# Where the output rows and the fast tiles of a feed-forward lie: two more tiles of each by Strassen's method, row products in equal units

## The reference, cut to what matters

```python
def swiglu(h, w_gate, w_up, w_down):
    return (jax.nn.silu(h @ w_gate) * (h @ w_up)) @ w_down

for l in range(2):
    x = x + 0.5 * swiglu(rms_norm(x, ffn1_norm[l]), ffn1_wg[l], ffn1_wu[l], ffn1_wd[l])
    ...                         # mixing stage
    x = x + 0.5 * swiglu(rms_norm(x, ffn2_norm[l]), ffn2_wg[l], ffn2_wu[l], ffn2_wd[l])
```

## Time and profile before

| | |
|---|---|
| median of 3 runs | 2541.45 us (2541.44 to 2541.8) |
| the profiled execution | 2541.64 us, its span 2539.8 us |
| TensorE busy | 2519.7 us, 13626 matmuls |
| weight loads busy | 2177.9 us |
| VectorE busy | 1834.5 us |
| ScalarE busy | 1143.8 us |
| GpSimd busy | 303.9 us |
| read from HBM | 241.84 MB |
| TensorE's granted clock | 1.000 of full speed |

### The profile page before, as it was taken

The page is one execution under the profiler, slowest core; times in us unless marked ns, Lnnn a source line. Parts: engine busy times, 40 slices in busy tenths (PEclk is TensorE's granted clock), DMA queues, the critical chain, the costliest instruction groups (busy, mean ns, idle before and its releaser), DMA issues.

```text
span 2539.8 us, 34207 instructions
## 1 busy us (share of the span) xinstructions
PE 2519.7 (99%) x13626; PEld 2177.9 (86%) x13626; DVE 1834.5 (72%) x2475; ACT 1143.8 (45%) x1771; POOL 303.9 (12%) x250
## 2 busy tenths in 40 slices
PE   8999999999999999999999999999999999999999
PEld 7899988888999889999888899997888888788887
DVE  8877767777778677776776777777999786642433
ACT  5434445444434454443553444445577535431332
POOL 4000001320000000000023000000186231100001
PEclk9999999999999999999999999999999999999999
DMA  5333333233333333333423333234332333233332
GB/s 154 99 101 93 97 102 92 75 101 90 103 97 100 109 97 95 95 112 93 108 59 100 92 88 110 86 112 127 84 74 75 125 91 109 83 108 100 91 100 83
DMA packets 488421, 248.27 MB, mean 98 GB/s; under 512 B 40385, under 2 KB 485062, under 8 KB 488006
## 3 DMA queue, kind: packets, MB, share of 16 engines
q1 hardware_dynamic: 487810, 245.76, 33.5%
q10 hardware_dynamic: 452, 0.32, 0.1%
HBM read 241.84 MB, written 4.19 MB: 97 GB/s over the span
## 4 chain that ended last, share of the span: by engine, by line
PE 95%; DVE 3%; ACT 1%; issue 0%; DMA 0%; POOL 0%; DVEq 0%; ACTq 0%
PE bank L704 8%; PE bank L706 8%; PE bank L705 8%; PE bank L785 6%; PE bank L784 6%; PE bank L783 6%; PE psS L804 6%; PE psS L805 6%; PE psS L806 6%; PE psT L704 4%; PE psT L705 4%; PE psT L706 4%; PE psT L870 2%; PE psT L872 2%; PE psT L871 2%; PE psS L704 1%
## 5 line engine op out<-in xcount | busy, mean ns | idle before, releaser
L2004 DVE TENSOR_TENSOR wlo<-raw,whi 128x1024 fp32r<-128x1024 f32 (+1 forms) x274 | 362.0, 1323 | 114.8 <-ACT whi L1422 111.6
L704 PE MATMUL bank<-xhi,whi 128*128 128x512 f32 x888 | 349.3, 393 | 1.5 <-issue 1.5
L705 PE MATMUL bank<-xlo,whi 128*128 128x512 f32 x888 | 345.9, 390 | 0.0
L706 PE MATMUL bank<-xhi,wlo 128*128 128x512 f32 x888 | 345.8, 389 | 0.0
L1422 ACT ACTIVATE whi<-raw 128x1024 fp32r<-128x1024 f32 (+1 forms) x271 | 277.4, 1026 | 131.9 <-PE psT L706 92.4
L1454 ACT ACTIVATE whi<-tw 128x1024 fp32r<-128x1024 f32 x112 | 119.0, 1062 | 234.4 <-PE bank L785 205.8
L804 PE MATMUL psS<-hhi,whi 128*128 128x512 f32 x512 | 201.7, 394 | 0.0
L805 PE MATMUL psS<-hlo,whi 128*128 128x512 f32 x512 | 201.5, 394 | 0.0
L806 PE MATMUL psS<-hhi,wlo 128*128 128x512 f32 x512 | 199.2, 389 | 0.0
L704 PEld LDWEIGHTS bank<-xhi,whi 128*128 128x128 f32 x888 | 166.8, 188 | 36.8 <-issue 2.9
L705 PEld LDWEIGHTS bank<-xlo,whi 128*128 128x128 f32 x888 | 166.7, 188 | 35.1 <-issue 1.4
(11 more groups left out here) (596 smaller groups left out, 6498.6 us busy)
## 6 DMA issues: line engine op xcount, KB each, us to landing
raw<-in_ffn_wg SPq DMA_DIRECT2D x88, 512.0 KB
raw<-in_ffn_wu SPq DMA_DIRECT2D x88, 512.0 KB
raw<-in_ffn_wd SPq DMA_DIRECT2D x96, 384.0 KB
raw<-in_w_mlp SPq DMA_DIRECT2D x64, 512.0 KB
raw<-in_w_in SPq DMA_DIRECT2D x53, 512.0 KB
raw<-in_ffn_wd SPq DMA_DIRECT2D x32, 256.0 KB
raw<-in_w_in SPq DMA_DIRECT2D x24, 256.0 KB
raw<-in_w_out SPq DMA_DIRECT2D x11, 512.0 KB
```

Source lines behind the costliest of these rows:

```text
L704: pe.matmul(dest, a, rhs_hi(k), start=start and k == 0, stop=False)
L705: pe.matmul(dest, a, rhs_lo(k), start=False, stop=False)
L706: mm = pe.matmul(dest, b_, rhs_hi(k), start=False, stop=stop and k == tiles - 1)
L2004: dve.tensor_tensor(wlo[:, a:a + n], raw[:, a:a + n], whi[:, a:a + n].bitcast(F32), ALU.subtract).then_inc(s_split, 1)
```

## The change

The list of windows goes. The three plain windows stay (tiles 0 to 5), and each of the other 16 tiles has a fast window: FAST = 16 instead of 14, no mixed ones. GROUPS become 6, 6, 5 and 5 tiles. The output rows of a group are laid out as one list of blocks (row by row, one 128 x 128 block of weights each), and `down_units` cuts that list into equal units, two for each window of the next group: 4 blocks a unit while group 0 and group 2 are worked off, 4 or 5 for group 1. So a row can begin in the middle of one unit and end in another, a row's bank of `psS` is chosen by m % 2 instead of by unit, and a unit that holds parts of two rows is loaded by two transfers. The waits for hidden tiles and for free banks move to single blocks, and a row is added where it ends. The last group has 5 tiles, so each row of `last_down` has 5 blocks where it had 6.

```diff
-    WINDOWS = [("plain", 0, None), ("plain", 2, None), ("plain", 4, None)]
-    GROUPS = [(0, 6), (6, 12), (12, 16), (16, FC)]
-    WINDOWS += [("mixed", 6, None)] + [("down", 8 + i, (0, 2 * i)) for i in range(KC // 2)]
-    WINDOWS += [("down", 12 + i, (1, 2 * i)) for i in range(KC // 2)]
-    WINDOWS += [("down", 16, (2, 0)), ("down", 17, (2, 2)), ("mixed", 18, None), ("down", 20, (2, 4)), ("down", 21, (2, 6))]
+    GROUPS = [(0, 6), (6, 12), (12, 17), (17, FC)]
+    FAST = FC - 2 * PLAIN
+
+    def down_units(grp, n):
+        rows = [(grp, m, k) for m in range(KC) for k in range(GROUPS[grp][1] - GROUPS[grp][0])]
+        return [rows[len(rows) * i // n:len(rows) * (i + 1) // n] for i in range(n)]
+
+    SIDES = []
+    for grp, (f0, f1) in enumerate(GROUPS[1:]):
+        units = down_units(grp, 2 * (f1 - f0))
+        SIDES += [units[2 * i:2 * i + 2] for i in range(f1 - f0)]
...
+        def side_cols(w, i):
+            return len(SIDES[w][i]) * P
+
+        def side_ends(w, i):
+            return [(grp, m) for grp, m, k in SIDES[w][i] if k == tiles_in(grp) - 1]
...
+                def side_rows(w, i):
+                    c = c0 + 4 * (PLAIN + w) + 2 + i
+                    slot_free(c, q0)
+                    unit = SIDES[w][i]
+                    chunks = sorted({(grp, m) for grp, m, k in unit})
+                    at_k = 0
+                    for grp, m in chunks:
+                        ks = [k for g_, m_, k in unit if m_ == m]
+                        k0 = GROUPS[grp][0] + ks[0]
+                        sp.dma_start(dst(c, at_k, at_k + len(ks)), cols(wd, l, k0, k0 + len(ks), m * P)
+                                     ).then_inc(landed[slot(c)], LANDED // len(chunks))
+                        at_k += len(ks)
...
-                def side_half(w, i, half, dest):
-                    kind, tile, side = WINDOWS[w]
-                    n = 4 if kind == "mixed" else tiles_in(side[0]) // 2
-                    for k in range(half * n, (half + 1) * n):
...
+                def side_half(w, i, half):
+                    unit = SIDES[w][i]
+                    cut = (len(unit) + 1) // 2
+                    for j in (range(cut, len(unit)) if half else range(cut)):
+                        grp, m, k = unit[j]
+                        if k == 0:
+                            if grp or m >= 2:
+                                pe.wait_ge(k_xa, nf * ADDS + grp * KC + m - 1)
+                            elif m == 0:
+                                pe.wait_ge(s_gs, fb + 2 * PLAIN)
+                        if m == 0:
+                            pe.wait_ge(s_hl, fb + GROUPS[grp][0] + k + 1)
+                        a, dest = (2 * i + 1) * UNIT + j * P, psS[:, m % 2 * S:(m % 2 + 1) * S]
+                        at_h, last = (GROUPS[grp][0] + k) % HT, k == tiles_in(grp) - 1
+                        pe.matmul(dest, whi[:, a:a + P], chunk(hhi, at_h), start=k == 0, stop=False)
+                        pe.matmul(dest, whi[:, a:a + P], chunk(hlo, at_h), start=False, stop=False)
+                        mm = pe.matmul(dest, wlo[:, a:a + P], chunk(hhi, at_h), start=False, stop=last)
                     return mm
...
-                for w, (kind, tile, side) in enumerate(WINDOWS):
-                    if kind == "plain":
-                        pair(q0 + 4 * w, fb + tile, w == 0)
-                    else:
-                        fast_window(w)
+                for w in range(PLAIN):
+                    pair(q0 + 4 * w, fb + 2 * w, w == 0)
+                for w in range(FAST):
+                    fast_window(w)
...
+                def side_adds(w, i):
+                    ends = side_ends(w, i)
+                    if ends:
+                        dve.wait_ge(s_used, q0 + c0 + 4 * (PLAIN + w) + 2 + 2 * i)
+                    for grp, m in ends:
+                        dve.scalar_tensor_tensor(chunk(x, m), psS[:, m % 2 * S:(m % 2 + 1) * S], 0.5, chunk(x, m), ALU.mult,
+                                                 ALU.add).then_inc(k_xa, 1)
```

More of the change, by code:

```diff
@@ L1551, in fast_window @@
                         last_hi(w + 1)
-                    hidden_hi(w, True)
-                for w, (kind, tile, side) in enumerate(WINDOWS):
-                    if kind == "plain":
-                        pair(w)
-                    else:
-                        fast_window(w)
+                    hidden_hi(w)
+                for w in range(PLAIN):
+                    pair(w)
+                for w in range(FAST):
+                    fast_window(w)
                 for m in range(KC):
@@ L2153, in hidden_lo @@
+                def hidden_lo(w):
+                    tile = 2 * PLAIN + w
                     dve.wait_ge(s_hh, fb + tile + 1)
-                    dve.tensor_tensor(chunk(hlo, tile % HT), tmp[3 if fast else 2][:, :], chunk(hhi, tile % HT).bitcast(F32),
+                    dve.tensor_tensor(chunk(hlo, tile % HT), tmp[3][:, :], chunk(hhi, tile % HT).bitcast(F32),
                                       ALU.subtract).then_inc(s_hl, 1)
                 def fast_window(w):
-                    kind, tile, side = WINDOWS[w]
@@ L2159, in fast_window @@
[L2159 removed]
+                    u, g, f = 4 * (PLAIN + w), nf * FAST + w, fb + 2 * PLAIN + w
                     c = q0 + c0 + u
[L2161 removed]
+                    on = w + 1 < FAST
                     t1, t2 = quarter
[L2163 to L2166 removed]
+                    if w:
+                        side_adds(w - 1, 1)
@@ L2167, in fast_window @@
                     whole_lo(w, 1)
-                    if before == "mixed":
-                        hidden_lo(w - 1, False)
                     dve.wait_ge(k_pe, 5 * g + 2)
@@ L2178, in fast_window @@
                         ahead(u + 4)
[L2179 to L2183 removed]
+                    side_adds(w, 0)
                     if on:
@@ L2207, in fast_window @@
                         last_lo(w + 1)
-                    hidden_lo(w, True)
-                for w, (kind, tile, side) in enumerate(WINDOWS):
-                    if kind == "plain":
-                        pair(w)
-                    else:
-                        fast_window(w)
-                side_add(len(WINDOWS) - 1, 1)
+                    hidden_lo(w)
+                for w in range(PLAIN):
+                    pair(w)
+                for w in range(FAST):
+                    fast_window(w)
+                side_adds(FAST - 1, 1)
                 for m in range(KC):
```

159 lines of the change are left out of this document (49 added, 110 removed).

## The result

| | before | after |
|---|---|---|
| median | 2541.59 us (13 runs, 2541.44 to 2542.06) | 2546.93 us (13 runs, 2546.57 to 2548.47) |
| ratio | | 1.0022, interval 1.0014 to 1.0029 |
| the profiled execution | 2541.64 us, span 2539.8 | 2548.21 us, span 2546.4 |

The kernel became 5.3 us slower. The forecast was 2546.7, slower by 5.1. After's runs stand at two levels: 7 of 13 at 2546.57 to 2546.93, 6 at 2548.12 to 2548.47; the profiled execution is one of the upper ones. The median is the highest run of the lower level, so it hangs on that seventh run. What the 1.5 us between the levels are is told with the experiment on it.

The account below looks back on a forecast made before the run. TensorE was taken as the bound, busy 2519.7 of 2539.8 us. Terms -5.76 + 10.6 + 0.2 = +5.1 us on the profiled 2541.64 gave 2546.7 us, 0.2% slower, own range 2545 to 2548, wider range 2543.5 to 2551.

Parts of the forecast that it names:

- Two more tiles by Strassen: In each of four feed-forwards, two plain tiles (10.88 us) become fast ones (10.16); eight tiles save 5.76 us of TensorE.
- Sixteen short windows, none stalls: Fast windows of each feed-forward: eleven at 15.60 us, five at 16.7 on average, nothing stalls, cost nothing.
- Rival C: Fast windows too short for weight transfers and vector work; 0.2 us more over 44 windows gives 2555 us; chance 0.08.
- The first window: First window of the first feed-forward: TensorE arrives 1.36 us sooner, splits shrink, stall stays about 1.6 us; cost 0.
- The tail: Output rows behind each last window: vector engine steps of 3.48, then 4.09 us make TensorE wait; 10.6 us lost in all.
- Behind the tail: Phase after the norm's sum: something with under 0.97 us to spare may lose it, three times; taken as 0.2 us.
- Rival B: Next phase follows the vector engine, losing all of the 0.97 us three times: 2549.4 us; chance 0.15.
- A: Rows behind the last window: vector step under TensorE's 3.40 us, 5.76 us earned in full: 2535.9 us; chance 0.10.
- D: First rows behind the last window overlap better, step 3.3 to 3.4 us, waits vanish: 2542 to 2544 us; chance 0.12.

## Why the prediction was right

*Two more tiles by Strassen, -5.76.* Shown by the three kernels whose tails and windows don't stall: 2535.96, 2536.03 and 2535.93, that is 5.8 to 5.9 us below the kernel before as timed beside each (2541.86, 2541.86 and 2541.76).

*Sixteen short windows, none stalls.* Right in all 64 but the first: 15.60, and 16.69 on average for the five (16.7 predicted). Rival C is wrong here, but near: with groups 6, 5, 5, 6 its wait appears in a window of 14.91 us. The lateness that I read was too small: the 0.28 us of one window became 0.16 to 1.45 us of wait for the up weights in every window but the first and the last of each feed-forward. The slack covered it: in the window from 258.62 VectorE still waits 1.69 us for TensorE, and in the one with 1.45, a window of 16.28 us, 1.19.

*The first window.* The stall was to stay at about 1.6 us, and is 1.66. The window took 17.34, 1.74 above 15.60; the fast windows begin at 79.84, 0.06 later than before.

*The tail.* Right in its steps. The additions' last came at 26.08 (26.09 predicted), row 7 at 18.64 (18.65), chunk 7 at 28.36 (28.39), the norm's sum at 29.17 (29.2). The wait at row 7 was 0.56 where I had 0.69, since TensorE lost 0.13 in restarts on the way and came later; at chunk 7 it was 1.43 (1.5), behind the second feed-forward 2.14 (2.3), with the product that waits for x high starting 27.57 after the first addition (27.6). In sum 10.9 by two runs, where I had 10.6. One reading was wrong without harm to the sum: I wrote that the last three splits are of 1024-column weights, and ahead of the mixing stage half of these columns hold nothing that is used.

*The reason I gave for its pace* was half right. I wrote that VectorE is working off its own chain. With 640 columns that holds within 0.11 us of 3.48; with 1024 columns the circle over ScalarE is as long, and work taken from VectorE buys nothing. The sum came out because its steps were read from the distances of additions, which hold both engines' parts. As a guide to a cure the reason misled: it made me expect 2535.8 of a kernel that took 2560.53.

*Behind the tail, +0.2.* The fast windows of the next three feed-forwards begin 1.12, 4.51 and 5.49 us later than before. By my terms it is 1.09, 2.86 and 3.89; the second has 1.65 more, which is the fallen clock of the profiled execution, and the rest agrees within 0.1. Rival B did not come; 27 us behind the last row of the fourth one TensorE starts 0.2 us late, at 1780.59. The end is 6.6 us later, 5.1 in the executions of the lower level. The fallen clock is no term of the sum: had one more of the 13 runs had it, the median would stand at the upper level, 1.4 us above the forecast. That it stands within 0.3 is luck to that extent; the lower level, 2546.70 in the middle, is what was forecast.

*Rivals A and D.* A needed a step under 3.40 and is what the moved split brings about; in the kernel as changed it was 3.48 and 4.09. D needed 3.3 to 3.4; the run with narrow splits shows it, 3.35, where both waits go.

## What to carry to other kernels

Work taken from the engine that sets the end is earned only down to the step of the serial chain beside it: before such a cut, read the distance between the chain's repeats, and compare it with what the engine will need per repeat. When a chain goes to and fro between engines, look for an operation in it that nobody in the chain waits for, and put it where one engine waits for the other: here the same work in another order was worth 10.9 us. Units of side work should be even: the mean length of the windows was the same, yet one window of 14.91 us in each feed-forward stalled, where sixteen of 15.60 did not. And a helper's default size deserves a look: half of each wide split ahead of the mixing stage was work that nobody read, and to leave it out of after was worth 4.3 us.

## What the runs showed of the hardware

*TensorE's clock fell behind a single short wait.* In the profiled execution of after the granted clock was 0.50 from 889.0 us for 3.4 us, 1.2 instead of 2.4 GHz, while TensorE was busy throughout; a wait of 2.14 us had ended at 888.09. From the matmul at 888.66 sixteen took 5.26 us where they take 3.63 at full clock: 1.6 us more, about the 1.5 us between the two levels. 6 of 13 runs stood at the upper level, and none of 11 with the wait filled; that filling this wait takes the upper level away is shown by that. The waits of 1.43 us behind the other feed-forwards brought no fall in this execution. Why it comes in one execution and not in the next is open, and the length of the wait alone doesn't settle it: in the profiled run with the sums on GpSimd the four waits for chunk 7 were 2.0, 2.4, 2.0 and 2.0 us, and the clock fell to 0.50 behind the third and the fourth only. That is a part of that run's 13.6 us over after.

*GpSimd's additions lengthened VectorE's.* An operation of VectorE with two operands in SBUF took 1.45 us for 0.83, and 1.52 for 1.23, beside an addition of GpSimd. The Trainium skill, "SBUF — State Buffer", section Who interferes with whom, says that such an operation and a GpSimd operation that reads SBUF exclude each other, and the later one waits for the end of the earlier. The rows agree to 0.14 us: GpSimd's addition began first, at 348.60, and ended at 348.60 + 1.29 = 349.89; 0.83 behind that is 350.72, and the split ended at 350.58.
